# The order of VectorE's work in a Mamba-2 group loop, and the order of its ring of weight loads

## Chip, core and metric

The kernel runs on one core of one Trainium2 chip. The metric is the device time of one execution in microseconds (us). Before the change it is 2198.63 us, the median of three runs (2197.93 to 2201.19).

## The reference, cut to what matters

One layer over 256 latent tokens and 256 context tokens, width 2048, in float32: adaLN modulation and RMSNorm, a bidirectional Mamba-2 mixer (64 heads in 8 groups of 8, state 128), a gated residual, a second norm, and a two-level mixture of experts.

```python
mx = modulation(c, ada_w, ada_b)            # silu(c) @ w + b, cut in six
hx = modulate(rms_norm(x, g), mx[0], mx[1]) # and hc from ctx
z, xbc, dt = split(h @ w_in)                # per group of heads: z 512, x 512, B 128, C 128 columns
xbc = silu(centred_dwconv(xbc, conv_w, conv_b))   # three taps over time
# per direction: the context's final state, then the latents
w = (C B^T) * exp(cum_i - cum_j) * dt       # masked to the triangle
y = w @ x + (C * exp(cum)) @ state + D * x
y = rms_norm(y * silu(z), norm_g) @ w_out
x = x + mx[2] * y
x = x + mx[5] * hier_moe(modulate(rms_norm(x), mx[3], mx[4]))
```

`mx[2]` to `mx[5]` come from the last two thirds of `ada_w`; they are needed only after the mixer.

## The kernel before, in words

The stages, in order: a front (norms, the first third of `ada_w`, dt and the first projection), the group loop, the output projection, routing, and a loop over experts that streams their weights.

The group loop runs `steps(g, w, ssd)` on each engine, for g = 0 (only weights, `w`), 1 to 7 (weights of group g and the SSD work, `ssd`, of group s = g - 1) and 8 (SSD of group 7 beside the first output tiles). A group has ten weight chunks of 128 columns, `CHUNKS`: 0 is B, 1 is C, 2, 5, 8, 9 are x, and 3, 4, 6, 7 are z. B and x chunks are projected for 512 tokens, C and z for 256. Each chunk is 1 MB of `w_in`, loaded to one of the three slots of `raw`.

A float32 product is made of three passes in a rounded format: ScalarE copies the weights rounded (`conv_hi`, L706, tile `whi`), VectorE subtracts to get the residue (`conv_lo`, `lo`, L955, tile `wlo`), and TensorE (`project`, L1585 and L1586, then L1590) runs the high weights against both parts of the activations and then the low weights against the high part. `whi` and `wlo` have two slots each. ScalarE's first convolution tap (`conv_first`, L724) and VectorE's other two (L1098, L1101 in `drain`) leave PSUM; for z chunks `drain` is one multiplication (L1090). ScalarE takes a tanh, VectorE finishes the silu (`store`, L998).

Beside the chunks, in each group:
- The second and third part of the modulation: eight tiles "a" of `ada_w`, 1 MB each, in the same three slots. `ada_sum(g, j)` (L1226, L1229) multiplies a tile's four rows of columns into `arow` on VectorE; after four tiles TensorE's `ada_columns` (L1669) sums over the partitions, and VectorE's (L1235) adds the bias.
- The SSD work: `differences` (L1027, VectorE, 16 instructions), `decays` (L774 and L779, ScalarE's exponentials), `weights` (L1037 and L1041, VectorE), each in two halves; `scaled_x` (L1055 to L1058), `states` and `y_chunk` 0 to 3 on TensorE, `finish` (L1066 to L1072) on VectorE, and `y_stores` on GpSimd's queue.

Every engine's order within a step n is written out by hand. TensorE: chunk n, then `states` at step 2, `y_chunk` 0 and 1 at step 3, 2 and 3 at step 6. They wait for `weights` of the half (`s_wts`, `s_ce`). ScalarE: `conv_hi` of the next chunk first, then the decays at steps 0 and 4, then tanh and first tap. VectorE: `conv_lo` of the next chunk first, then the rest.

`LOADS` is the order in which SP issues the 18 loads of a group: ten "w" and eight "a". The one at position p takes slot p mod 3, and waits until the load three positions earlier is used up: a "w" by its `conv_lo` (`s_lo`), an "a" by its `ada_sum` (`s_aadd`). SP is in order, so a load also waits for those ahead of it. After the last group the same slots take tiles of `w_out`, and SP issues `y_load`, which brings back `yh` and `yl` (0.5 MB each per group), between them; the first output tile on TensorE (`out_tile`, L1688) waits for both parts of group 0. The second of them is issued when the last chunk of the loop is done.

Of the kernel before, what the change touches and what calls it, by code (L numbers as in the profile page):

```python
# [36 lines left out]
NCH = len(CHUNKS)  # L37
# [7 lines left out]
ADDS = [4 * j + 4 for j in range(NADA)]  # L45
NADD = ADDS[-1]

ADA_STEP = {0: 0, 1: 1, 2: 2, 3: 3, 5: 4, 6: 5, 7: 6, 8: 7}
LOADS = [("w", 0)] + [t for n in range(NCH - 1) for t in [("w", n + 1)] + ([("a", ADA_STEP[n])] if n in ADA_STEP else [])]
RAW = 3  # L50
SLOTS = 64

# [1 line left out]
def build(nc, t):  # L54
# [70 lines left out]
    with ExitStack() as ctx:  # L125
# [170 lines left out]
        s_prod = sem("s_prod")  # L296
# [364 lines left out]
        def _(act):  # L661
# [38 lines left out]
            def conv_hi(g, n):  # L700
                m = NCH * g + (n + 1)
                pos = POS[("w", n)]
                act.wait_ge(s_raw[raw_of(pos)], raw_count(group_raw(g), pos))
                if not (isinstance(g, int) and g == 0 and n == 0):
                    act.wait_ge(s_wh, m - 1)
                act.activation(whi[:, (n + 1) % 2, :], raw[:, raw_of(pos), :], ACT.Copy).then_inc(s_hi, 1)  # L706
# [74 lines left out]
            def steps(g, w, ssd):  # L781

                s = g - 1
                for n in range(NCH):
                    if w and n + 1 < NCH and not (isinstance(g, int) and g == 0 and n < 2):
                        conv_hi(g, n + 1)
                    if w and n + 1 == NCH:
                        if not (isinstance(g, int) and g == GROUPS - 1):
                            conv_hi(g + 1, 0)
                        else:  # L790
                            out_hi(0)
                    if not w and n == 0:
                        tanh_of(s, NCH - 1)
                        turn_store(s, 8)
                    if not w and n != 3:
                        out_hi(n + 1)
                    if not w and n == 2:
                        out_hi(4)
                    if ssd and n in (0, 4):
                        decays(s, n // 4)  # L800
                    if n > 0 and w:
                        tanh_of(g, n - 1)
                    if n == 0 and ssd and w:
                        tanh_of(s, NCH - 1)
                    if w and n in CONV_AT:
                        if not (isinstance(g, int) and g == 0 and n == 0):
                            conv_first(g, n)
                    if ssd and n == 0 and w:
                        turn_store(s, 8)
                    if ssd and n == 1:  # L810
                        turn_store(s, 9)
                    if ssd and n == 2:
                        act.wait_ge(s_st, s + 1)
                        act.activation(st[:, 0, :], STK[0][:, :], ACT.Copy)
                        act.activation(st[:, 1, :], STK[1][:, :], ACT.Copy).then_inc(s_stev, 1)
                    if w and n in (2, 4, 7):
                        turn_store(g, {2: 0, 4: 2, 7: 5}[n])
# [60 lines left out]
        def _(dve):  # L878
# [205 lines left out]
            def drain(g, n):  # L1084

                kind = CHUNKS[n][0]
                slot, bank = n % 2, banks[(n + 1) % 2]
                if kind == "z":
                    dve.wait_ge(s_win, NCH * g + (n + 2))
                    dve.tensor_scalar(cv[:, slot, 0:L], bank[:, 0:L], 0.5, None, ALU.mult).then_inc(s_drain, 1)  # L1090
                    return
                q = 2 if kind in "Bx" else 1
                o = cv[:, slot, 0:q * L].rearrange("p (q t) -> p q t", q=q)
                u = bank[:, 0:q * L].rearrange("p (q t) -> p q t", q=q)
                col = conv_col(g, n)
                i = NCONV * g + (CONV_AT[n] + 1)
                dve.wait_ge(s_cvA, i)
                dve.scalar_tensor_tensor(o[:, :, 1:L], u[:, :, 0:L - 1], tapc[:, 0, bass.ds(col, 1)], o[:, :, 1:L],  # L1098
                                         ALU.mult, ALU.add).then_inc(s_cvB, 1)
                dve.wait_ge(s_cvB, i)  # L1100
                dve.scalar_tensor_tensor(o[:, :, 0:L - 1], u[:, :, 1:L], tapc[:, 2, bass.ds(col, 1)], o[:, :, 0:L - 1],  # L1101
                                         ALU.mult, ALU.add).then_inc(s_drain, 1)
# [39 lines left out]
            def steps(g, w, ssd):  # L1142
                s = g - 1
                for n in range(NCH):
                    if ssd and w and n == 4:
                        finish(s, 0)
                        finish(s, 1)
                        differences(s, 1)
                    if w and n + 1 < NCH and not (isinstance(g, int) and g == 0 and n < 2):
                        conv_lo(g, n + 1)  # L1150
                    if w and n + 1 == NCH:
                        if not (isinstance(g, int) and g == GROUPS - 1):
                            conv_lo(g + 1, 0)
                        else:
                            out_lo(0)
                    if not w and n not in (0, 2, 3):
                        out_lo(n)
                    if not w and n == 1:
                        dve.wait_ge(s_ads, 2 * GROUPS)
                        dve.tensor_copy(a2c, adab[:, ADA1:ADA1 + ADA2]).then_inc(s_a2, 1)  # L1160
                        dve.wait_ge(s_a2, 1)
                        dve.scalar_tensor_tensor(a2c[:, 2 * KC:3 * KC], a2c[:, 2 * KC:3 * KC], 1.0, g1col, ALU.add, ALU.mult).then_inc(s_a2, 1)
                    if not w and n == 3:
                        dve.wait_ge(s_a2T, 1)
                        dve.tensor_copy(a2row, ADAK[0:ADA2, 0:P]).then_inc(s_a2r, 1)
                    if not w and n == 0:
                        store(s, NCH - 1)
                    if ssd and n == 0:
                        dve.tensor_copy(tokg[:, :, :, :], tokm[:, :, :, bass.ds(R * s, R)]).then_inc(s_tg, 1)
                        dve.wait_ge(s_prod, NCH * s + 2)  # L1170
                        dve.tensor_copy(cT2[:, :], cT[:, :]).then_inc(s_ct2, 1)
                        dve.wait_ge(s_tg, s + 1)
                        differences(s, 0)
                    if not w and n == 4:
                        finish(s, 0)
                        finish(s, 1)
                        differences(s, 1)
                    if w and n == 6:
                        ada_columns(g, 0)
                    if ssd and n == 7:  # L1180
                        finish(s, 2)
                        finish(s, 3)
                    if ssd and n == 0:
                        if w:
                            store(s, NCH - 1)
                        skip_term(s, 8)
                    if w and n > 0:
                        store(g, n - 1)
                    if ssd and n == 1:
                        skip_term(s, 9)  # L1190
                    if w and n == 4:
                        skip_term(g, 2)
                    if w and n == 7:
                        skip_term(g, 5)
                    if not w and n == 1:
                        out_lo(2)
                        scaled_x(s)
                        out_lo(3)
                    if ssd and w and n == 1:
                        scaled_x(s)  # L1200
                    if ssd and (n == 5 or (n == 1 and not w)):
                        weights(s, n // 5)
                    if w and n == 8:
                        masked(g)
                    if w and not (isinstance(g, int) and g == 0 and n == 0):
                        drain(g, n)
                    if isinstance(g, int) and g == 0 and n == 2:
                        dt_columns()
                    if w and n == 9:
                        ada_columns(g, 1)  # L1210
                    if ssd and w and n == 1:
                        weights(s, 0)
                    if w and n in ADA_STEP:
                        ada_sum(g, ADA_STEP[n])

            def ada_sum(g, j):
# [288 lines left out]
        def _(pe):  # L1505
# [187 lines left out]
            def steps(g, w, ssd):  # L1693
                s = g - 1
                for n in range(NCH):
# [25 lines left out]
                        y_chunk(s, 1 if n == 3 else 3)  # L1721
                    if w and n == 7:
                        c_times_b(g)
                    if w and n in (5, 9):
                        ada_columns(g, n // 9)

            steps(0, True, False)
            with pe.Fori(1, GROUPS - 1) as g:
# [164 lines left out]
```

## Time and profile before

| | us |
|---|---|
| median of 3 runs | 2198.63 (2197.93 to 2201.19) |
| profiled execution, span from first to last instruction | 2195.6 |
| TensorE busy | 1980.9 (90%) |
| VectorE busy | 1228.3 (56%) |
| ScalarE busy | 496.7 (23%) |
| GpSimd busy | 153.7 (7%) |
| mean rate of the DMA over the span | 304 GB/s |

The page gives no other time of the profiled execution than its span; the median of the runs lies 3.0 us above it, for what lies around the first and the last instruction. The group loop runs from about 133 to 997 us, the output projection to about 1205, the experts from about 1249 on. In the profile PE is TensorE's matmuls, DVE VectorE, ACT ScalarE, POOL GpSimd, SPq the queue from which SP issues loads. PEclk is the granted TensorE clock as a share of full speed. A number in brackets at the end of a timeline row is the idle time ahead of it, with what ended it.

### The profile page before, as it was taken

The page shows a single profiled execution, that of the slowest core. Times are in us where ns is not written, and L with a number is a line of the kernel's source. Part 1 is how long each engine was busy: PE and PEld are TensorE (multiplying, and loading weights), DVE is VectorE, ACT ScalarE, POOL GpSimd, SP SyncE. Part 2 cuts the span into 40 slices and gives each one's busy share as a digit, 9 for nine tenths or more (in the row PEclk, how much of TensorE's full clock was granted, in tenths as well). Part 3 has the DMA queues.
Part 4 walks back from the last instruction along what each step waited for, and adds up shares of the span by engine and source line. Part 5 has one row for each costly group of instructions (what it writes and reads, how often), then busy time and mean ns, then how long its engine had stood idle before and what let it go on. Part 6 is the DMA issues. An engine that isn't in the chain of part 4 may idle for free.

```text
span 2195.6 us, 27594 instructions
## 1 busy us (share of the span) xinstructions
PE 1980.9 (90%) x10090; PEld 1228.5 (56%) x10090; DVE 1228.3 (56%) x1999; ACT 496.7 (23%) x577; POOL 153.7 (7%) x214
## 2 busy tenths in 40 slices
PE   5768999999999999999998798999988889989888
PEld 2358788888787878787787533333333333333333
DVE  2367788888888888888784623333222233322234
ACT  3123333333333333335444300000000000000000
POOL 0000000000000000000691000000000000000000
PEclk9789999999999999999999899999999999999999
DMA  9958576767676767679672699999999999999997
GB/s 361 313 171 246 164 219 184 221 183 218 189 214 190 214 190 212 192 221 310 231 236 91 268 426 426 427 427 427 426 426 426 426 426 427 427 427 426 425 426 288
DMA packets 294718, 666.68 MB, mean 304 GB/s; under 512 B 13505, under 2 KB 188001, under 8 KB 261009
## 3 DMA queue, kind: packets, MB, share of 16 engines
q1 hardware_dynamic: 285728, 639.45, 78.1%
q0 software_dynamic: 7984, 26.40, 3.7%
q8 instruction: 28, 0.46, 0.1%
q10 hardware_dynamic: 960, 0.23, 0.1%
q14 instruction: 18, 0.14, 0.0%
HBM read 655.40 MB, written 10.65 MB: 303 GB/s over the span
## 4 chain that ended last, share of the span: by engine, by line
DMA 28%; PE 17%; POOL 4%; DVE 1%; issue 1%; SPq 1%; ACT 0%; DVEq 0%; POOLq 0%
DMA wt<-in_moe_w_up 28%; PE bank L1831 12%; PE bank L1688 2%; POOL ysq L638 1%; POOL ysq L645 1%; POOL ysq L643 1%; PE bank L1856 1%; SPq L529 1%; PE bank L1795 0%; PE bank L1796 0%; PE bank L1813 0%; PE bank L1747 0%; PE bank L1788 0%; PE bank L1740 0%; DVE x L1465 0%
## 5 line engine op out<-in xcount | busy, mean ns | idle before, releaser
L1831 PE MATMUL bank<-wt,xe 128*64 128x512 f32 x1984 | 468.0, 627 | 80.5 <-DMA wt<-in_moe_w_up 80.5
L1465 DVE TENSOR_TENSOR x<-x,bank 128x512 f32<-128x512 f32 x256 | 158.3, 680 | 536.0 <-PE bank L1813 536.0
L1585 PE MATMUL bank<-hTh,whi 128*128 128x256 f32 (+1 forms) x1264 | 408.0, 343 | 16.4 <-ACT whi L706 14.1
L1586 PE MATMUL bank<-hTl,whi 128*128 128x256 f32 (+1 forms) x1264 | 401.0, 337 | 0.0
L1831 PEld LDWEIGHTS bank<-wt,xe 128*64 128x64 f32 x1984 | 164.1, 144 | 381.0 <-issue 380.9
L1585 PEld LDWEIGHTS bank<-hTh,whi 128*128 128x128 f32 x1264 | 241.8, 191 | 47.6 <-ACT whi L706 15.9
L1590 PE MATMUL bank<-hTh,wlo 128*128 128x256 f32 (+1 forms) x1264 | 240.8, 346 | 18.3 <-DVE wlo L955 18.3
L1586 PEld LDWEIGHTS bank<-hTl,whi 128*128 128x128 f32 x1264 | 242.1, 192 | 23.6
L1590 PEld LDWEIGHTS bank<-hTh,wlo 128*128 128x128 f32 x1264 | 204.5, 199 | 44.5 <-DVE wlo L955 20.1
L1856 PE MATMUL bank<-wt,hdn 128*64 128x512 f32 x1024 | 226.8, 595 | 1.4 <-DVE hdn L1477 1.4
L706 ACT ACTIVATE whi<-raw 128x2048 fp32r<-128x2048 f32 x80 | 153.1, 1914 | 302.3 <-DMA raw<-in_ssm_w_in 285.0
L955 DVE TENSOR_TENSOR wlo<-raw,whi 128x2048 fp32r<-128x2048 f32 x80 | 183.0, 2288 | 60.4 <-ACT whi L706 60.1
L867 ACT ACTIVATE gsb<-bank 128x512 f32<-128x512 f32 x32 | 19.1, 597 | 835.9 <-PE bank L1831 835.9
L1229 DVE SCALAR_TENSOR_TENSOR arow<-raw,cvec,arow 128x512 f32<-128x512 f32 x240 | 180.0, 750 | 6.8
L1856 PEld LDWEIGHTS bank<-wt,hdn 128*64 128x64 f32 x1024 | 70.7, 137 | 153.0 <-issue 127.9
L1813 PE MATMUL bank<-osb,gTb 64*128 64x512 f32 x512 | 138.1, 622 | 1.7 <-DVE osb L1494 1.7
L965 DVE SCALAR_TENSOR_TENSOR wlo<-raw,packs,whi 128x512 fp32r<-128x512 f32 x128 | 113.5, 947 | 34.1 <-ACT whi L757 34.1
L1494 DVE TENSOR_TENSOR osb<-bank,gate_h 128x512 f32<-128x512 f32 x64 | 41.2, 685 | 109.3 <-PE bank L1856 109.3
L757 ACT ACTIVATE whi<-raw,packs 128x512 fp32r<-128x512 f32 x128 | 81.9, 712 | 81.8 <-issue 58.9
L1813 PEld LDWEIGHTS bank<-osb,gTb 64*128 64x128 f32 x512 | 53.5, 185 | 65.4 <-issue 48.2
L1688 PE MATMUL bank<-whi,yh 128*128 128x512 f32 x256 | 66.4, 402 | 4.4 <-issue 2.9
L774 ACT ACTIVATE wts<-wts 128x3072 f32<-128x3072 f32 x16 | 44.4, 2776 | 99.3 <-DVE wts L1027 99.3
(304 smaller groups left out, 1837.9 us busy)
## 6 DMA issues: line engine op xcount, KB each, us to landing
wt<-in_moe_w_gate SPq DMA_DIRECT2D x64, 2048.0 KB, 16.6
wt<-in_moe_w_up SPq DMA_DIRECT2D x64, 2048.0 KB, 21.1
wt<-in_moe_w_down SPq DMA_DIRECT2D x64, 2048.0 KB, 18.5
raw<-in_ssm_w_in SPq DMA_DIRECT2D x80, 1024.0 KB, 6.1
raw<-in_ada_w SPq DMA_DIRECT2D x70, 1024.0 KB, 6.2
raw<-in_ssm_w_out SPq DMA_DIRECT2D x32, 1024.0 KB, 5.1
fr<-in_ada_w SPq DMA_DIRECT2D x26, 1024.0 KB, 11.6
bc<-cum_d POOLq DMA_DIRECT2D x32, 512.0 KB, 4.9
```

The costliest lines, as they stand in the source:

```text
L706: act.activation(whi[:, (n + 1) % 2, :], raw[:, raw_of(pos), :], ACT.Copy).then_inc(s_hi, 1)
L955: dve.tensor_tensor(wlo[:, slot, :], raw_tile, whi[:, slot, :].bitcast(F32), ALU.subtract).then_inc(s_lo, 1)
L965: last = dve.scalar_tensor_tensor(wlo[:, m % 2, cols], raw[:, raw_of(OUT0 + i), cols], ngcol[:, 4 * q + j:4 * q + j + 1], whi[:, m % 2, co ...
L1229: dve.scalar_tensor_tensor(arow[:, :], tile[:, i, :], column, arow[:, :], ALU.mult, ALU.add).then_inc(s_aadd, 1)
L1465: dve.tensor_tensor(x1[:, tt, cols], x1[:, tt, cols], banks[(1, 3, 6, 7)[nb]][:, :], ALU.add).then_inc(s_acc2, 1)
L1585: pe.matmul(bank[:, 0:width], wh[:, k, :], hTh[:, k, 0:width], start=(k == 0), stop=False)
L1586: last = pe.matmul(bank[:, 0:width], wh[:, k, :], hTl[:, k, 0:width], start=False, stop=False)
L1590: last = pe.matmul(bank[:, 0:width], wl[:, k, :], hTh[:, k, 0:width], start=False, stop=(k == KC - 1))
L1688: last = pe.matmul(banks[2 * nb + tt][:, :], a[:, 4 * q + j, P * tt:P * tt + P], ring[:, m % 2, 512 * j:512 * j + 512], start=(q == 0 and ...
L1813: pe.matmul(banks[(1, 3, 6, 7)[nb]][:, :], gTb[rows, P * tt:P * tt + P], osb[rows, nb // 2, :], start=True, stop=True).then_inc(s_cm[nb % ...
L1831: last = pe.matmul(banks[0][SLOTS * h:SLOTS * h + SLOTS, :], rows[:, k, :], wt[2 * q + h][:, FF * i:FF * i + FF], start=(k == 0), stop=(k ...
L1856: last = pe.matmul(banks[4 + nb // 2][SLOTS * h:SLOTS * h + SLOTS, :], hdn[:, f, :], wt[2 * NQ + f // 2][:, D * (f % 2) + 512 * nb:D * (f ...
```

## The change

It touches the three orders and nothing that is computed. It adds one wait.

- `LOADS` is written out in another order: w0 w1 a0 w2 w3 a1 w4 a2 w5 w6 a3 w7 a4 w8 a5 w9 a6 a7, where it was w0 w1 a0 w2 a1 w3 a2 w4 a3 w5 w6 a4 w7 a5 w8 a6 w9 a7.
- ScalarE: `conv_hi` of chunk 6 moves from the start of step 5 to step 4, ahead of the second `decays`.
- VectorE: `ada_sum(0)` goes behind the first `differences` of step 0 (in group 0 it stays at the step's end). `conv_lo` of chunk 3 goes from the start of step 2 to the end of step 1, ahead of `ada_sum(1)`. In step 4, `drain` of chunk 4, `conv_lo` of chunk 6 and the second `weights` come right behind `conv_lo` of chunk 5 and ahead of the stores; `weights` were in step 5. `ada_sum` 3 to 7 move to steps 5, 6, 7, 8 and 9 (they were in 3, 5, 6, 7 and 8), those of steps 5 and 9 ahead of `drain`. The first `ada_columns` go to step 7 on VectorE and step 6, behind `y_chunk`, on TensorE.
- `drain` of a z chunk waits for the store two chunks back as well (`s_prod`).

```diff
-ADA_STEP = {0: 0, 1: 1, 2: 2, 3: 3, 5: 4, 6: 5, 7: 6, 8: 7}
-LOADS = [("w", 0)] + [t for n in range(NCH - 1) for t in [("w", n + 1)] + ([("a", ADA_STEP[n])] if n in ADA_STEP else [])]
+LOADS = [("w", 0), ("w", 1), ("a", 0), ("w", 2), ("w", 3), ("a", 1), ("w", 4), ("a", 2), ("w", 5),
+         ("w", 6), ("a", 3), ("w", 7), ("a", 4), ("w", 8), ("a", 5), ("w", 9), ("a", 6), ("a", 7)]
+ADA_STEP = {1: 1, 2: 2, 5: 3, 6: 4, 7: 5, 8: 6, 9: 7}
+COLS_AT = {6: 0, 9: 1}
...
 # ScalarE, steps
-                    if w and n + 1 < NCH and not (isinstance(g, int) and g == 0 and n < 2):
+                    if w and n + 1 < NCH and n != 5 and not (isinstance(g, int) and g == 0 and n < 2):
                         conv_hi(g, n + 1)
+                    if w and n == 4:
+                        conv_hi(g, 6)
...
 # VectorE, drain of a z chunk
                     dve.wait_ge(s_win, NCH * g + (n + 2))
+                    dve.wait_ge(s_prod, NCH * g + (n - 1))
...
 # VectorE, steps
-                    if w and n + 1 < NCH and not (isinstance(g, int) and g == 0 and n < 2):
+                    if w and n + 1 < NCH and n not in (2, 5) and not (isinstance(g, int) and g == 0 and n < 2):
                         conv_lo(g, n + 1)
+                    if w and n == 4:
+                        drain(g, 4)
+                        conv_lo(g, 6)
+                        if ssd:
+                            weights(s, 1)
...
                         differences(s, 0)
+                        if w:
+                            ada_sum(g, 0)
...
-                    if w and n == 6:
-                        ada_columns(g, 0)
                     if ssd and n == 7:
                         finish(s, 2)
                         finish(s, 3)
+                    if w and n == 7:
+                        ada_columns(g, 0)
...
-                    if ssd and (n == 5 or (n == 1 and not w)):
+                    if not w and n in (1, 5):
                         weights(s, n // 5)
...
+                    if w and n in (5, 9):
+                        ada_sum(g, ADA_STEP[n])
-                    if w and not (isinstance(g, int) and g == 0 and n == 0):
+                    if w and n != 4 and not (isinstance(g, int) and g == 0 and n == 0):
                         drain(g, n)
...
                     if ssd and w and n == 1:
                         weights(s, 0)
-                    if w and n in ADA_STEP:
+                    if w and n == 1:
+                        conv_lo(g, 3)
+                    if w and not ssd and n == 0:
+                        ada_sum(g, 0)
+                    if w and n in (1, 2, 6, 7, 8):
                         ada_sum(g, ADA_STEP[n])
...
 # TensorE, steps
-                    if w and n in (5, 9):
-                        ada_columns(g, n // 9)
+                    if w and n in COLS_AT:
+                        ada_columns(g, COLS_AT[n])
```

## Rows read from the trace of the kernel before

**Rows 1.** Busy time by stretch: window, length, engines busy, PEclk, DMA share, GB/s.

```profile
341.87:451.35 109.48, 104.20 (x625) 88.18 (x624) 91.56 (x141) 39.97 (x38) 6.54 (x12) 0.97 0.68 202
...
1250.00:2195.60 945.60, 856.64 (x3714) 306.83 (x3710) 280.77 (x498) 31.39 (x64) 0.00 (x0) 0.97 0.99 417
```

**Rows 2.** Waits in the loop, 232 to 997 us: total us, times, longest.

```profile
PE bank L1590 <- DVE wlo L955: 18.3, 7, 2.8
...
PE bank L1640 <- issue: 16.2, 7, 2.3
...
PE bank L1585 <- ACT whi L706: 2.0, 7, 0.6
```

**Rows 3.** TensorE's timeline, low part of chunks 3 and 4: start, us, what.

```profile
380.72 3.44 PE L1590 MATMUL bank<-hTh,wlo 128*128 128x256 f32 x16 [2.69 <-DVE wlo L955]
...
392.73 2.08 PE L1590 MATMUL bank<-hTh,wlo 128*128 128x256 f32 x16
```

**Rows 4.** Busy time by stretch, around four waits of TensorE (PE column first).

```profile
380.00:388.00 8.00, 7.28 (x56) 5.89 (x58) 6.60 (x9) 2.43 (x2) 0.00 (x0) 0.79 0.91 275
412.00:421.00 9.00, 6.67 (x55) 4.77 (x55) 8.74 (x9) 0.63 (x1) 0.00 (x0) 0.81 0.23 90
184.92:194.00 9.08, 9.08 (x40) 7.53 (x41) 5.83 (x6) 2.96 (x4) 0.00 (x0) 1.00 1.05 316
1150.00:1165.00 15.00, 8.72 (x32) 7.00 (x31) 5.90 (x10) 3.27 (x6) 9.27 (x12) 0.70 0.41 140
```

**Rows 5.** VectorE's timeline in that group.

```profile
355.61 0.69 DVE L998 SCALAR_TENSOR_TENSOR slx<-slx,cv 128x512 f32<-128x512 f32 x1 [5.15 <-ACT slx L745]
...
375.36 3.10 DVE L1229 SCALAR_TENSOR_TENSOR arow<-raw,cvec,arow 128x512 f32<-128x512 f32 x4
378.38 2.28 DVE L955 TENSOR_TENSOR wlo<-raw,whi 128x2048 fp32r<-128x2048 f32 x1
...
407.23 2.29 DVE L955 TENSOR_TENSOR wlo<-raw,whi 128x2048 fp32r<-128x2048 f32 x1 [1.26 <-ACT whi L706]
...
409.77 3.42 DVE L1037 TENSOR_TENSOR wts<-wts,cbm 128x1536 f32<-128x1536 f32 x2
```

**Rows 6.** ScalarE's timeline: second exponentials, and the copy for chunk 6.

```profile
400.03 2.78 ACT L774 ACTIVATE wts<-wts 128x3072 f32<-128x3072 f32 x1 [5.96 <-DVE wts L1027]
...
405.29 1.91 ACT L706 ACTIVATE whi<-raw 128x2048 fp32r<-128x2048 f32 x1
```

**Rows 7.** The group's loads (L481), issue to landing.

```profile
DMA to landing us min/median/max: 5.1/6.1/8.9
```

**Rows 8.** VectorE's timeline at the group's end: a tap of chunk 8, its store.

```profile
441.06 0.74 DVE L1098 SCALAR_TENSOR_TENSOR cv<-bank,tapc,cv 128x510 f32<-128x510 f32 x1
...
449.50 0.68 DVE L998 SCALAR_TENSOR_TENSOR slx<-slx,cv 128x512 f32<-128x512 f32 x1
```

**Rows 9.** Timeline of group 0: SP's loads, a copy on ScalarE, chunks 3 and 5.

```profile
133.77 0.37 SPq L481 DMA_DIRECT2D raw<-in_ada_w  x1
157.40 0.37 SPq L481 DMA_DIRECT2D raw<-in_ssm_w_in  x1
...
166.83 1.91 ACT L706 ACTIVATE whi<-raw 128x2048 fp32r<-128x2048 f32 x1 [11.70 <-DMA raw<-in_ssm_w_in]
...
168.80 0.58 PE L1585 MATMUL bank<-hTh,whi 128*128 128x256 f32 x1 [10.08 <-ACT whi L706]
...
184.92 0.50 PE L1585 MATMUL bank<-hTh,whi 128*128 128x512 f32 x1 [2.09 <-ACT whi L706]
```

**Rows 10.** After the loop: a `y_load`, two waits of TensorE, landings of `yl`.

```profile
996.70 0.37 SPq L492 DMA_DIRECT2D yl<-yl_d  x1
...
1000.82 2.07 PE L1688 MATMUL bank<-whi,yh 128*128 128x512 f32 x8 [2.86 <-issue]
...
1018.86 1.98 PE L1623 MATMUL bank<-xwf,btok 128*128 128x512 f32 x4 [0.86 <-DVE xtok L1058]
...
DMA to landing us min/median/max: 4.0/10.7/13.2
```

## The prediction

> **What bounds the kernel now.** I read the stages first [rows 1]. From 1250 us on, the expert loop keeps the DMA at 0.99 of its time and 417 GB/s. It starts when the stage before it ends and the change touches nothing in it, so what is won or lost earlier moves the end one for one. The group loop (eight groups; the last seven carry the SSD work of the group before them) costs 109.48 us a group: TensorE is busy 104.2 of them, VectorE 91.6, the DMA 0.68. TensorE bounds it, so only its waits can be won. The list of waits [rows 2] has three of TensorE in the loop, each seven times: for a low part `wlo` 18.3 us in all (2.6 each), ahead of `y_chunk` 16.2 (2.3), for a `whi` 2.0 (0.3). Together 5.2 us a group.
>
> The timeline shows a second price [rows 3]: the 16 low matmuls behind the first wait took 3.44 us, the same 16 of the next chunk 2.08. The granted clock was 0.79 over those 8 us and 0.81 around the `y_chunk` wait [rows 4], a piece at 1.2 in place of 2.4 GHz each time: 0.21 x 8 and 0.19 x 9, 1.7 us each. Over a whole group it is 0.97 [rows 1], 3.3 us. So the waits cost 5.2 + 3.3 = 8.5 us a group, and a group without them takes 101.0.
>
> The Trainium skill (TensorE: Matmul & The Clock Gate, HAM oscillation — how this bites in real kernels) says that a long enough operand wait drops the engine to half rate and that the loop pays the return each time; the trace agrees [rows 3, 4]. By waits alone seven groups would give 36 us; with the clock they give 60.
>
> Why the waits are there: VectorE, in order. In step 3 the residue of `z0` starts at 378.38, right behind an `ada_sum` that ran 375.36 to 378.46 [rows 5]; its copy `whi` was long done. TensorE waited for it. In step 5 the residue of chunk 6 waits 1.26 us for its `whi`, which ScalarE makes only after both exponentials [rows 6]; behind it stand the second `weights`, which free `y_chunk` 2 at 415.4.
>
> **The change, part by part.** I count from the start of a group's chunk 0 on TensorE (341.87 = 0). Without waits TensorE starts chunk 1 at 11.3, 2 at 17.5, `states` at 28.5, 3 at 32.1 (its low part at 36.0), y 0 and 1 at 38, chunk 4 at 42.5 (low 46.4), 5 at 48.8 (low 56.1), 6 at 60.6 (low 64.5), y 2 and 3 at 66.5, 7 at 71.0 (low 74.9), 8 at 78.0, 9 at 89.1, and ends it at 100.0. The times below add up start-to-start durations of the same group's timeline, a few of which stand in rows 5, 6 and 8.
>
> (a) `ada_sum(0)` moves in front of the store of the last chunk. VectorE idles 5.15 us there (at 355.61) [rows 5], so its 2.75 us are covered, if its tile has landed. The tile is now loaded after `ada_sum(7)` of the group before, issued about -0.8; with the median landing of 6.1 [rows 7] it is there at 5.3, `differences` end at 7.2. Cover holds.
>
> (b) `conv_lo(3)` goes ahead of `ada_sum(1)`, and `w3` is loaded right after `w2`. With (a), VectorE finishes the first `weights` at 29.6 instead of 33.5; the residue ends at 31.8, TensorE wants it at 36.0. The 2.6 us wait goes. Next behind: `ada_sum(1)` to 34.8, drain(2) to 36.7, then `ada_sum(2)`, whose tile follows `conv_lo(3)` in the ring: issued 32, landed 38.1. VectorE waits 1.4 us (new), ends at 41.1, and `conv_lo(4)` at 43.3 against 46.4.
>
> (c) Step 4: finish 0 and 1, second `differences` to 51.3, `conv_lo(5)` to 53.5 (wanted 56.1), drain(4), `conv_lo(6)` to 56, second `weights` (3.34 + 2.20) to 61.6; y 2 wants them at 66.5. ScalarE makes `whi` of chunk 6 before the exponentials: its load follows `conv_lo(4)`, 43.5 + 6.1 = 49.6, copy to 51.5, exponentials 51.5 to 56. The 2.3 us wait goes, and so does the 0.3 for a `whi` (ready at 51.5, wanted at 60.6). The smallest slack left is 2.6 us, at chunk 5.
>
> (d) The added wait of drain for `s_prod` names a store two chunks back, done more than 2 us before in every step walked here: nothing.
>
> (e) `ada_sum(7)` now ends in step 9 and TensorE's second `ada_columns` waits for it. TensorE leaves chunk 8 at 89.1; ScalarE's first tap 0.9, drain(8) 1.55, `ada_sum(6)` 3.0, residue of the next chunk 0 2.2, store 0.6, `ada_sum(7)` 3.0 [rows 5, 8]: 100.4, against 100.0. If `w0` lands later than the median (it shares the queue with `a7`), the residue starts later: 8.9 instead of 6.1 [rows 7] gives 2.5 us. Bounds 0.3 and 2.5; I take 0.8, near the median. Behind a wait of 2.09 us at 184.92 [rows 9] the granted clock was 1.00 [rows 4], so I add nothing for it. Each drain(9) and the next group's start then stand as before.
>
> (f) Group 0. TensorE waits 10.08 us for `whi` of chunk 3, because its load is issued only after `ada_sum(0)` (157.40) and lands at 166.7 beside two more [rows 9]. Now `w3` follows `conv_lo(1)` at 133.8, so chunk 3 starts behind drain(1) at 159.2. But the tiles `a1`, `a2`, `w4` come after `ada_sum(0)` as before, and `ada_sum(1)` and `ada_sum(2)` stand ahead of `conv_lo(4)`: 166.7 + 3.0 + 2.9 + 3.0 + 2.2 = 177.8, so chunk 4 waits about 4 us and ends at 179.7 to 180.7 (was 182.2). Chunk 5 then loses its 2.09 us wait. Gain 1.5 to 6, I take 3.
>
> (g) The end. The output phase's third weight tile takes the slot of `a7`, no longer of `w8`, and SP issues it before `y_load(0)`. Before, `y_load`'s second half went at 996.70, landed in 4.0 us, and TensorE started at 1000.82, 4.3 after its last chunk [rows 10]. Now `ada_sum(7)` of the last group also stands behind `out_lo(0)` (2.7 us, fed by a 2.5 us copy) and ends 2.5 us after the last chunk; then 1.05 MB of weights, 0.52 and 0.52 MB go out in a row. 2.1 MB at 417 GB/s [rows 1] is 5.0 us, some 5.6 with loads of two kinds mixed, plus the 2.6 that a 4.0 us landing leaves beside the 1.4 of its own 0.52 MB: TensorE starts 10.8 after its last chunk, 6.5 later; 0.86 of it is absorbed by the wait at 1018.86. Another idle stretch, 15 us of which TensorE worked 8.7, went with a granted clock of 0.70 [rows 4], so I add 1.5 to 3 for clock. Bounds: 0 (if `ada_sum(7)` were as early as `w8` before) and 10; I take 7.5.
>
> The DMA page of the Trainium skill (DMA: Bandwidth & Descriptors, Queues, rings and completion order) says that each DMA engine consumes a queue's descriptors in ring order, which speaks against this change: the small loads wait behind the megabyte. The `yl` rows agree, 4.0 us with nothing ahead and a median of 10.7 in the backlog. Were they independent, (g) would cost some 4 us in place of 7.5.
>
> **Sum.** Seven groups x -8.5 = -59.5; (e) in six, +4.8; (f) -3; (g) +7.5: -50.2 us. The profiled execution spans 2195.6, 3.0 under the median shown; the same difference goes on top: 2195.6 - 50.2 + 3.0 = 2148.4, 2148 us.
>
> **The rivals.**
> R1, the wait of (e) becomes a restart: `w0` lands late behind `a7` and the `bc` loads, TensorE waits 2.5 us and the clock falls (1.7), as at the two waits removed. 4.2 in place of 0.8, in six groups: +20, 2168. For: longest landing 8.9 in the group walked. Against: the median.
> R2, one of the two waits stays: slack 2.6 at chunk 5, 3.1 at chunk 4, both behind the ring's chain. One wait is 2.6 + 1.7: +30, 2178. For: (b) makes VectorE wait for `a2`. Against: 2 to 5 us of slack everywhere.
> R3, slower: the ring binds. `conv_lo(3)`, load `a2`, `ada_sum(2)`, `conv_lo(4)`, load `w6`, its copy, exponentials, `weights`, y 2 form one chain with two landings. It has 4.9 us to spare. If each landing took 13.2 as in the output phase's backlog [rows 10], it would end 14.2 late and TensorE would wait 9.3 in all, 4 at chunk 4 and 5.3 ahead of y 2, and lose 1.7 of clock twice: 12.7 against the 8.5 won, +4.2 in seven groups and +9.3 from (e) to (g): 2237. It decides from landings of some 11 us. Against: 8.9 at most here, and DMA at 0.68.
> R4, nothing moves: another wait of the same length appears, 2199. Nothing in the walk shows one.
>
> **Chances.** Forecast 0.75, R1 0.10, R2 0.08, R3 0.04, R4 0.03. Range 2135 (no cost in (g), 6 in (f)) to 2174 (R1, and half of R2). 0.2% is 4.4 us, about what this kernel's runs can tell from nothing: faster 0.93, same 0.03, slower 0.04.
>
> **What would show it.** Per group: 101 to 102 us; no TensorE wait for `wlo` and none ahead of `y_chunk`; a granted clock near 1.00 in the loop; a wait ahead of L1669's matmuls of 0.3 to 1 us, in the second `ada_columns` only; in group 0 chunk 3 at about 159 with a wait in chunk 4; an idle TensorE of 6 us or more ahead of the first output tile. The forecast is wrong if a group takes over 104 us, or if ScalarE's second exponentials start later than 52 after the group's start.

## The result, and the profile after

The changed kernel takes 2179.1 us (median of 4 runs, 2174.7 to 2182.6) against 2199.7 (four runs now, 2197.9 to 2201.2; the first three had 2198.6): a ratio of 0.9905, 95% interval 0.9893 to 0.9917. It is 20.6 us faster, where 50 were forecast, and outside the range given. The profiled execution spans 2173.2 us against 2195.6. It is the fastest of the four, 4.4 us below their median; the medians carry the result, the traces the account of it.

Both old waits of TensorE are gone: the list of its waits from 232 to 997 us (total us, times, longest) has one line of the loop, and it is a new one; the other is the first output tile.

```profile
PE bank L1687 <- DVE arow L1247: 22.9, 7, 3.5
PE bank L1706 <- issue: 6.5, 1, 6.5
```

L1687 is the second `ada_columns`, which waits for `ada_sum(7)`, 3.0 to 3.5 us in each of the last seven groups. The timeline of the end of one group (start, us, what; `...` stands for rows left out) shows how that wait comes about:

```profile
418.02 0.55 POOL L601 DMA_DIRECT2D bc<-cum_d  x1 [0.23 <-issue]
418.75 0.55 POOL L601 DMA_DIRECT2D bc<-cum_d  x1 [0.18 <-issue]
...
420.24 0.37 SPq L483 DMA_DIRECT2D raw<-in_ada_w  x1
...
422.47 9.74 SPq L483 DMA_DIRECT2D raw<-in_ssm_w_in  x2
...
428.57 3.11 DVE L1247 SCALAR_TENSOR_TENSOR arow<-raw,cvec,arow 128x512 f32<-128x512 f32 x4
...
432.24 1.92 ACT L708 ACTIVATE whi<-raw 128x2048 fp32r<-128x2048 f32 x1 [5.39 <-DMA raw<-in_ssm_w_in]
...
434.19 2.29 DVE L959 TENSOR_TENSOR wlo<-raw,whi 128x2048 fp32r<-128x2048 f32 x1 [2.52 <-ACT whi L708]
436.40 0.68 DVE L1002 SCALAR_TENSOR_TENSOR slx<-slx,cv 128x512 f32<-128x512 f32 x1
...
437.00 3.11 DVE L1247 SCALAR_TENSOR_TENSOR arow<-raw,cvec,arow 128x512 f32<-128x512 f32 x4
...
440.24 1.05 PE L1687 MATMUL bank<-ones,arow 128*128 128x1 f32 x8 [3.48 <-DVE arow L1247]
...
441.15 0.58 PE L1603 MATMUL bank<-hTh,whi 128*128 128x512 f32 x1
...
441.53 0.63 PE L1604 MATMUL bank<-hTl,whi 128*128 128x512 f32 x1
```

Read it from below. TensorE waits 3.48 us for the sum that VectorE began at 437.00. That sum stands behind a store and the residue at 434.19, and this residue idled 2.52 us for ScalarE's `whi`. ScalarE itself had waited for the load of `w0`, issued at 422.47: 9.8 us to the start of its copy. The same load took 7.7 before the change (issued 437.60, copy at 445.34). The load of `a7`, issued at 420.24, landed 8.4 us later, 8.3 ahead of its sum; VectorE can't reach that sum past the blocked residue.

What `w0` waited for stands in the DMA's view. A row of this weight chunk is 512 bytes long. From 422.5 to 426.5 no packet of that size moved (the packets below 2 KB are the 23 below 512 bytes):

```profile
DMA packets 489, 1.19 MB, mean 299 GB/s; under 512 B 23, under 2 KB 23, under 8 KB 489
...
q1 hardware_dynamic: 349, 0.71, 50.8%
q0 software_dynamic: 140, 0.48, 37.7%
```

SP's queue (q1) was moving `a7`, which `w0` stands behind, and GpSimd's (q0) took over a third of the engines' time beside it.

Behind the wait, TensorE runs slowly. Busy time by stretch (columns as in rows 1), the group and two starts of chunk 0:

```profile
335.12:441.15 106.03, 102.55 (x625) 87.10 (x624) 91.69 (x142) 40.13 (x37) 6.55 (x12) 0.98 0.70 208
...
441.15:444.55 3.40, 3.40 (x11) 2.62 (x11) 3.09 (x5) 0.00 (x0) 0.00 (x0) 0.53 0.92 296
```

A granted clock of 0.53 is the 1.2 GHz level, but for a remainder: matmuls of 0.63 us in place of 0.39. Chunk 0's high part takes 8.96 us instead of 7.36, so the wait costs 1.6 more. Without both the group would take 100.9, close to the 100.7 that e1 below measures.

**Where the 22.4 us of span come from**, taken between the second `ada_columns` of groups 0 and 7 (starts 231.44 and 996.51 before, 229.85 and 969.07 after): group 0 -1.6; seven groups 765.1 to 739.2, -25.9, or 109.3 to 105.6 each; from the last of them to the first output tile 4.3 to 8.1, +3.8; all that follows +1.2.

### The profile page after: what moved, and what is told of

Its sections match the earlier page's. It is cut to its first block, busy times and chain, and to the rows that moved or that the text cites. A ratio compares the mean times of both kernels' runs of the same rounds, so it can differ in the third digit from the quotient of the medians.

```text
span 2173.2 us, 27626 instructions
## 1 busy us (share of the span) xinstructions
PE 1974.7 (91%) x10090; PEld 1222.7 (56%) x10090; DVE 1229.5 (57%) x1999; ACT 498.0 (23%) x577; POOL 153.9 (7%) x214
## 4 chain that ended last, share of the span: by engine, by line
DMA 29%; PE 17%; POOL 4%; DVE 1%; issue 1%; SPq 1%; ACT 0%; DVEq 0%; POOLq 0%
DMA wt<-in_moe_w_up 29%; PE bank L1849 12%; PE bank L1706 2%; POOL ysq L640 1%; POOL ysq L647 1%; POOL ysq L645 1%; PE bank L1874 1%; SPq L531 1%; PE bank L1813 0%; PE bank L1814 0%; PE bank L1831 0%; PE bank L1765 0%; PE bank L1758 0%; PE bank L1806 0%; DVE x L1483 0%
## 5 line engine op out<-in xcount | busy, mean ns | idle before, releaser
L1603 PE MATMUL bank<-hTh,whi 128*128 128x256 f32 (+1 forms) x1264 | 413.7, 347 | 8.5 <-ACT whi L708 5.9
L1604 PE MATMUL bank<-hTl,whi 128*128 128x256 f32 (+1 forms) x1264 | 407.2, 342 | 0.0
L1608 PE MATMUL bank<-hTh,wlo 128*128 128x256 f32 (+1 forms) x1264 | 231.2, 335 | 0.2 <-DVE wlo L959 0.2
L1608 PEld LDWEIGHTS bank<-hTh,wlo 128*128 128x128 f32 x1264 | 196.8, 190 | 24.7 <-DVE wlo L959 0.4
L726 ACT ACTIVATE cv<-bank,tapc 128x512 f32<-128x512 f32 (+1 forms) x48 | 35.6, 742 | 169.7 <-PE bank L1608 134.3
```

What stands on the lines that cost most here:

```text
L1603: pe.matmul(bank[:, 0:width], wh[:, k, :], hTh[:, k, 0:width], start=(k == 0), stop=False)
L1604: last = pe.matmul(bank[:, 0:width], wh[:, k, :], hTl[:, k, 0:width], start=False, stop=False)
L1608: last = pe.matmul(bank[:, 0:width], wl[:, k, :], hTh[:, k, 0:width], start=False, stop=(k == KC - 1))
```

## The experiments

Every run was timed in three rounds beside the kernel before, whose medians were 2200.6 (first four) and 2198.7 (last four). "Period" is the mean over the seven groups of the profiled execution, between second `ada_columns`. After and e4 run the same code in the loop, so the 0.7 us between their periods is what two executions can differ by.

| kernel | median us | ratio, 95% interval | period us |
|---|---|---|---|
| before | 2199.7 | 1 | 109.30 |
| after | 2179.1 | 0.9905 (0.9893-0.9917) | 105.60 |
| last sum first (e1) | 2138.9 | 0.9721 (0.9704-0.9737) | 100.69 |
| `bc` loads later (e2) | 2162.4 | 0.9821 (0.9805-0.9837) | 103.79 |
| quarter of `a7` (e3) | 2129.9, not comparable | 0.9682 (0.9666-0.9699) | 102.87 |
| `y_load` first (e4) | 2174.5 | 0.9879 (0.9863-0.9896) | 106.31 |
| before + part (c) (p1) | 2175.1 | 0.9888 (0.9868-0.9908) | 105.24 |
| before + (b), old ring (p2) | 2216.9 | 1.0085 (1.0068-1.0101) | 111.36 |
| e1 without (a) (p3) | 2148.7 | 0.9773 (0.9756-0.9789) | 102.27 |
| e1 and e4 (e5) | 2136.8 | 0.9722 (0.9706-0.9738) | 100.69 |

### e1: `ada_sum(7)` ahead of the residue of the next group's chunk 0

```
                     if w and n + 1 == NCH:
+                        ada_sum(g, ADA_STEP[n])
                         if not (isinstance(g, int) and g == GROUPS - 1):
...
-                    if w and n in (5, 9):
+                    if w and n == 5:
                         ada_sum(g, ADA_STEP[n])
```

Expected: 

> Only VectorE's order in step 9 differs from the changed kernel: ada_sum(7) stands ahead of the residue of the next group's chunk 0 instead of behind it. Theory A (the new wait of 3.4 us ahead of the second ada_columns comes from the order: the sum is queued behind a residue that waits 2.5 us for its whi, whose load took 9.7 us): the sum ends about 2 us before TensorE's last chunk, the wait goes in all seven groups with the 1.6 us of clock behind it, a group takes 101 us, and the end's third weight tile comes earlier too: 2179 - 35 - 2 = about 2142. Theory B (the tile of the sum itself lands late, all loads at the group's end being slow): the wait stays at 1 us or more, 2165 or above.

Measured: 2138.9 us, 40 less than after, as theory A said. In the group's end of its trace both sums run back to back ahead of the residue:

```profile
418.23 8.71 SPq L483 DMA_DIRECT2D raw<-in_ssm_w_in  x2
...
423.30 6.26 DVE L1248 SCALAR_TENSOR_TENSOR arow<-raw,cvec,arow 128x512 f32<-128x512 f32 x8
427.49 1.92 ACT L708 ACTIVATE whi<-raw 128x2048 fp32r<-128x2048 f32 x1 [5.91 <-DMA raw<-in_ssm_w_in]
429.47 2.28 DVE L959 TENSOR_TENSOR wlo<-raw,whi 128x2048 fp32r<-128x2048 f32 x1
...
431.34 0.95 PE L1688 MATMUL bank<-ones,arow 128*128 128x1 f32 x8
```

`w0` is still late (9.3 us from issue to copy), and nobody waits for it: the residue ends at 431.75, and TensorE wants it at 439.51. 101 us around a group are filled without a gap at full clock:

```profile
330.00:431.00 101.00, 101.00 (x625) 86.31 (x624) 92.33 (x142) 40.02 (x37) 6.52 (x12) 1.00 0.74 219
```

So VectorE's order at the group's end is the cause of the missing gain: 4.9 us a group, 34 in the seven, and 2 more ahead of the first output tile. The profiled executions differ by 35.9 us, the medians by 40.2, since the one of after was 4.4 below its median.

### e2 and e3: why `w0` is late

e2 holds the `bc` loads of the next group back until ScalarE has made the copy fed by `w0`; e3 loads only a quarter of the tile of `ada_sum(7)`. e3 so computes another modulation, which sends tokens elsewhere: 1920 expert matmuls in place of 1984. Its total can't be compared; its groups can.

```
                 pool.wait_ge(s_ebc, 2 * s + 2)
+                pool.wait_ge(s_hi, NCH * s + (2 * NCH + 2))
                 load_bc(s + 1, 0)
```

```
+                    if kind == "a" and n == 7:
+                        sp.dma_start(a_view(raw_of(pos))[:, 0:1, :], src[:, 0:1, :]).then_inc(...)
+                        continue
```

Expected of e2: 

> The changed kernel, with GpSimd's queue issuing the two broadcast loads of bc for the next group (1 MB) only once ScalarE has copied the next group's chunk 0, so that they are not in flight beside the loads of a7 and w0. Theory C (these broadcasts make w0's landing 9.7 us instead of 6): it lands in 7 us or less, the wait ahead of the second ada_columns falls below 1 us, 2179 - 30 = about 2150. Theory D (it is a7 in the same ring, issued 2.3 us ahead): landing still about 9, 2175 to 2180. If both share it: about 8 us, wait 1 to 2, 2155 to 2170.

Expected of e3: 

> The changed kernel, with a7's load cut to one of its four rows of columns (three quarters of the tile are left out and the sum reads what the slot held; the last part of the modulation is wrong in the output). It is issued 2.3 us ahead of w0 in the same ring. Theory D: 0.79 MB less ahead of w0 is 2.4 us earlier, the wait falls to about 1 us and the clock's 1.6 come back, 2179 - 7 x 4 = about 2151. Theory C: w0 lands as late as before, 2175 to 2180.

Measured, the same load's issue and copy, and TensorE's wait, first e2:

```profile
424.27 9.73 SPq L483 DMA_DIRECT2D raw<-in_ssm_w_in  x2
...
430.90 1.92 ACT L709 ACTIVATE whi<-raw 128x2048 fp32r<-128x2048 f32 x1 [2.25 <-DMA raw<-in_ssm_w_in]
...
439.43 1.05 PE L1688 MATMUL bank<-ones,arow 128*128 128x1 f32 x8 [0.86 <-DVE arow L1248]
```

then e3:

```profile
420.78 9.73 SPq L486 DMA_DIRECT2D raw<-in_ssm_w_in  x2
...
428.79 1.92 ACT L711 ACTIVATE whi<-raw 128x2048 fp32r<-128x2048 f32 x1 [3.64 <-DMA raw<-in_ssm_w_in]
...
436.79 1.05 PE L1690 MATMUL bank<-ones,arow 128*128 128x1 f32 x8 [1.73 <-DVE arow L1250]
```

6.6 us in e2 and 8.0 in e3, against 9.8: in these groups the `bc` broadcasts account for 3.1 us and three quarters of `a7` for 1.8. So neither theory alone holds; 2162.4 lies in the range expected for a shared cause. No run takes both away. 9.8 less both is 4.9, near the 5.1 of the fastest load in rows 7, which leaves little for a third cause. The walk's 0.8 for step (e) was right for the landing it assumed: at 6.6 us the wait is 0.86. But other groups of e2 still wait up to 2.2, and it has a new wait, seen in its list of the loop's waits, because the held-back `bc` loads, issued at 433.53 and 434.26, now meet that of `w1` (433.63), which takes 9.2 us to land instead of 5.7, and VectorE's and ScalarE's work behind it comes late to the copy of chunk 2:

```profile
PE bank L1688 <- DVE arow L1248: 10.6, 8, 2.2
PE bank L1604 <- ACT whi L709: 3.5, 3, 1.2
```

Moving the loads gives back 1.8 us a group; moving one sum on VectorE gives 4.9.

### e4: `y_load(0)` ahead of the third output tile

```
+                if i == RAW - 1:
+                    sp.wait_ge(s_wh, M_OUT)
+                    y_load(0, 0)
+                    sp.wait_ge(s_win, M_OUT)
+                    y_load(0, 1)
                 if i < RAW:
...
                 sp.dma_start(a_view(raw_of(OUT0 + i)), w_out[...]).then_inc(...)
-                if i == RAW - 1:
...
```

Expected: 

> The changed kernel, with SP issuing both halves of the first y_load ahead of the third output weight tile. If the 7.2 us between the loop's last work on TensorE and the first output tile is the megabyte ahead in the ring, it falls back to about 3.5 to 4.5, and a piece at half clock goes: 3 to 6 us less, about 2175. If the wait has another cause (the stores of the rows themselves), it stays at 7 and the time at 2179.

Measured: 2174.5, 4.6 us less than after. After the loop SP of the changed kernel issued the megabyte first, and TensorE's first output tile waited (two views of after, SP's queue and TensorE):

```profile
969.04 0.37 SPq L507 DMA_DIRECT2D raw<-in_ssm_w_out  x1
969.52 0.44 SPq L494 DMA_DIRECT2D yh<-yh_d  x1
970.07 0.44 SPq L494 DMA_DIRECT2D yl<-yl_d  x1
...
977.20 3.32 PE L1706 MATMUL bank<-whi,yh 128*128 128x512 f32 x7 [6.54 <-issue]
```

In e4 both halves of `y_load(0)` go out at 967.97 and 971.60, before the weights at 974.30, and the tile starts right behind the loop:

```profile
974.33 1.05 PE L1687 MATMUL bank<-ones,arow 128*128 128x1 f32 x8 [2.76 <-DVE arow L1247]
975.24 0.63 PE L1631 MATMUL bank<-ident,slx 128*128 128x128 f32 x4
975.77 3.37 PE L1706 MATMUL bank<-whi,yh 128*128 128x512 f32 x8
```

So the wait was SP's order, as step (g) said: the first output tile starts 1.4 us behind the last `ada_columns` instead of 8.1. How much of these 6.7 us the kernel keeps isn't shown. What follows takes 1.2 longer, and the profiled spans are nearly equal, 2172.9 against 2173.2, since in e4's execution a group took 0.7 us more. The medians differ by 4.6, but the intervals of the two ratios overlap.

### p1: the kernel before with part (c) alone

ScalarE's copy of chunk 6, VectorE's drain, residue 6 and second `weights` move to step 4 as in the change; ring, residue 3 and sums stay.

Expected: 

> The kernel before with one part of the change alone, part (c): in each group the second set of decay weights is made behind the second exponentials, with ScalarE's copy of chunk 6's high weights and VectorE's residue of chunk 6 ahead of it; the old orders of the residues of chunks 3 and 4, of the sums of the modulation and of the weight ring stay. Theory (each of the two old waits of TensorE pays by itself): the second one goes, 2.33 us a group and 0.26 beside it, with the half-clock piece of 1.6 us behind it, 4.2 us a group, 7 groups: 2200.6 - 29 = 2171. Rival (the gain of this part is in the first wait's shadow, or the sum for chunk 7 becomes late also here): a gain of less than 10 us, 2190 or more.

Measured: 2175.1, no worse than the whole change. The loop's list has only the first old wait:

```profile
PE bank L1598 <- DVE wlo L957: 19.7, 9, 2.7
```

The period falls by 4.06 us, where waits and clock were priced at 4.2. 28.4 us in the groups; 1.6, 1.2 and 2.1 are given back in group 0, ahead of the first output tile and behind it.

### p2: part (b) with the old ring

```
-                    if w and n + 1 < NCH and not (isinstance(g, int) and g == 0 and n < 2):
+                    if w and n + 1 < NCH and n != 2 and not (isinstance(g, int) and g == 0 and n < 2):
                         conv_lo(g, n + 1)
...
+                    if w and n == 1 and not (isinstance(g, int) and g == 0):
+                        conv_lo(g, 3)
```

Expected: 

> The kernel before with VectorE's half of part (b) alone: the residue of chunk 3 goes ahead of the sum of the modulation for chunk 1, and the weight ring keeps its old order, in which the load of chunk 4's weights follows the release of that sum's buffer. Theory (order of the ring is needed for the order of VectorE): that load is issued 2.2 us later than before, its copy ends at about 388.8 us of the old profile where TensorE wants it at 384.3: TensorE waits some 4.5 us for the weights of chunk 4, instead of 2.7 for the residue: about 2210, no faster than before. Rival (VectorE's order alone does it): the wait and its clock go, 4.2 us a group: 2171.

Measured: 2216.9, slower than before. The residue runs earlier, but the sum of chunk 1, whose buffer chunk 4's weights take, now ends later (timeline, VectorE's residue and sum, SP, ScalarE, TensorE):

```profile
379.06 2.28 DVE L955 TENSOR_TENSOR wlo<-raw,whi 128x2048 fp32r<-128x2048 f32 x1
...
381.26 3.11 DVE L1233 SCALAR_TENSOR_TENSOR arow<-raw,cvec,arow 128x512 f32<-128x512 f32 x4
...
384.53 0.37 SPq L481 DMA_DIRECT2D raw<-in_ssm_w_in  x1
...
390.57 1.91 ACT L706 ACTIVATE whi<-raw 128x2048 fp32r<-128x2048 f32 x1 [12.22 <-DMA raw<-in_ssm_w_in]
...
392.53 0.58 PE L1589 MATMUL bank<-hTh,whi 128*128 128x256 f32 x1 [4.48 <-ACT whi L706]
```

4.48 us for `whi`, as worked out, in place of 2.6 for `wlo`. The total is 7 us above the 2210 expected: the seven groups lose 14.4 us, group 0 and what follows the loop another 4. VectorE's order and the ring's are one change: without its half in the ring the other half loses 2.1 us a group.

### p3: e1 without part (a)

```
                         differences(s, 0)
-                        if w:
-                            ada_sum(g, 0)
...
-                    if w and not ssd and n == 0:
+                    if w and n == 0:
                         ada_sum(g, 0)
```

Expected: 

> The version with the last sum of the modulation ahead of chunk 0's residue of the next group (2138.9 us), without part (a): the sum for chunk 0 goes back to the end of the step before, ahead of chunk 3's drain. Theory (VectorE's slack after part (b) is about as large as one sum, so part (a) is worth about 1.3 us a group): chunk 4 waits 0.8 us and chunk 5 1 to 2 us: about 2148. Rival (slack covers it): 2139, no change against that version.

Measured: 2148.7, 9.8 over e1, by a period 1.6 longer. No wait of over 0.4 us is left in its loop from 230 to 940 us, but 19 short ones, 5.1 us in all. In one group TensorE is idle 1.27 us, where e1's isn't idle at all:

```profile
330.50:433.50 103.00, 101.73 (x625) 86.07 (x623) 92.01 (x142) 39.95 (x38) 6.55 (x12) 1.00 0.72 214
```

That group takes 2.3 us longer than e1's; the part beyond the 1.27 isn't resolved by the profile, in which the ends of matmuls are modelled.

### e5: e1 and e4 together, the fastest version

Expected: 

> The version with the last sum of the modulation ahead of chunk 0's residue of the next group (2138.9 us), and with the load of the first y tile issued ahead of the third output tile after the loop, as in the run of that edit alone. Theory (the two are independent): the first output tile starts about 2 to 4 us sooner after the loop: 2135 to 2137. Rival (what is left of the wait after the loop is something else): 2139.

Measured: 2136.8 (2134.5 to 2139.4), beside e1's 2138.9 (2138.3 to 2139.7). The first output tile starts 4.2 us after the last `ada_columns` in place of 6.1, but the two sets of runs overlap. It beats after by 42 us and before by 62; nearly all of that is e1's.

## Why the prediction was wrong, step by step

**Right: what the two waits were worth.** With no wait left in the seven groups (e1) a group takes 100.69 us, 8.6 less than before; 8.5 was forecast, 5.2 of waits and 3.3 of clock. p1 shows the second wait by itself at 4.1.

**Right: (a), (b), (c), (d).** Neither old wait is left, and no other has come up between chunk 0 and chunk 9. In after, the residue of chunk 3 starts 31.3 us into the group (29.6 was said), the new wait of `ada_sum(2)` for its tile is 0.46 where 1.4 was said, and ScalarE's second exponentials start at 387.43, 52.3 into a group that begins at 335.12; 1.6 of that is the slow start of chunk 0. That passes the 52 which was to be the mark of a wrong forecast, and harmed nothing: the walk's slacks of 2 to 5 us held it. (a) is needed, as p3 shows (9.8 us), and so is the ring (p2).

**Wrong: (e), the second `ada_columns` waits for `ada_sum(7)`.** It was priced at 0.8 us a group, between bounds of 0.3 and 2.5, with nothing for the clock: +4.8 in six groups. It waited 3.0 to 3.5 us and cost 4.9 a group with the clock (after less e1), 34.4 in seven. The forecast had the last group's wait in (g); without its 3.5 the cost is 30.9 against 4.8, 26 of the 28 us by which the span missed. The mechanism was named, in the step and as R1 with 2.5 + 1.7 us; R1 got 0.10. Two choices failed. The landing of `w0` was taken at the median of the group's 18 loads, while this very load had taken 7.7 us, and the change itself puts `a7` ahead of it on the queue, beside the `bc` loads; it landed after 9.6, more than the 8.9 behind the upper bound. Step (g) reckoned with a queued megabyte after the loop; step (e) didn't a few lines earlier. Then the clock: it was left out because of the one wait of 2.09 us without a drop (rows 9), though waits of 2.3 and 2.7 us in the same trace had one (rows 4). So being 2.5 us wrong in the wait cost 4.1. Here a small error was not small.

The Trainium skill (DMA: Bandwidth & Descriptors, Queues, rings and completion order) says that each DMA engine switches in turn between the queue rows that hold work for it, a packet at a time; so a load on SP's queue gives up time to one from GpSimd though their queues differ. The trace agrees: in e2, with only the `bc` loads moved, `w0` needs 6.6 us instead of 9.8. Most of the difference passes through `a7`: `w0`'s first packet moves 4.1 us after its issue in after and 1.9 in e2.

**Half right: (f).** Group 0 gains 1.6 of the forecast 3: chunk 3 starts at 160.44 as said (about 159), but chunk 4 waits 5.89 where 4 was said.

**Right: (g).** The forecast counted from TensorE's last chunk, with the last wait for `ada_sum(7)` in it. That chunk ends at 965.60 in after, and the first output tile starts at 977.20: 11.6 us, where 10.8 was said, or 7.3 more than before. With the 1.2 behind it (g) costs 8.5 against 7.5, and e4 confirms the mechanism.

**The sum anew,** in the forecast's own terms: 7 x -8.6 = -60.3, (e) +30.9, (f) -1.6, (g) +8.5: -22.5, beside 22.4 measured in the span.

## What to carry to other kernels

On an in-order engine, don't queue work whose consumer is due now behind work that waits for a load and is due later: here one sum moved ahead of one residue is worth 36 us by the spans, 40 by the medians. When a walk gives a cost by a load's landing, take that load's own time and add what the change puts on the DMA ahead of it, not the median of all; and where the result is a wait of TensorE of 1 to 3 us, price it both with and without the clock. Two orders that share a ring of buffers (an engine's and the loads') must move together, or the buffer released later turns the gain into a loss.

## What the runs showed of the hardware

**A wait of TensorE can cost more than its length, and in these traces the length doesn't tell which one does.** The seven waits of 3.0 to 3.5 us in after were each followed by a piece at 1.2 GHz; five of 0.86 or 0.87 in e2 and e3 by none. Between them both happen. In e2 the same wait at the same place has two lengths in neighbouring groups. Behind 2.16 us the matmuls of the next chunk start at 0.63 us each, behind 0.86 at 0.39, and chunk 0's high part takes 10.2 us after the first, 2.8 more than after the second:

```profile
334.39 1.43 PE L1688 MATMUL bank<-ones,arow 128*128 128x1 f32 x8 [2.16 <-DVE arow L1248]
...
336.26 0.63 PE L1605 MATMUL bank<-hTl,whi 128*128 128x512 f32 x1
...
440.66 0.39 PE L1605 MATMUL bank<-hTl,whi 128*128 128x512 f32 x1
```

In e3 a wait of only 1.23 us came before such a piece, which cost 1.6 us; in p1 a wait of 2.68 us was followed by none, its 16 low matmuls taking 2.17 us where rows 3 has 3.44 behind 2.69. One row of each:

```profile
642.41 1.05 PE L1690 MATMUL bank<-ones,arow 128*128 128x1 f32 x8 [1.23 <-DVE arow L1250]
...
643.90 0.63 PE L1606 MATMUL bank<-hTh,whi 128*128 128x512 f32 x1
```

```profile
483.04 2.17 PE L1598 MATMUL bank<-hTh,wlo 128*128 128x256 f32 x16 [2.68 <-DVE wlo L957]
```

What else decides stays open.

**A load can stand still while the DMA as a whole is below its full rate.** In the 15 us around the late `w0` (418 to 433) the DMA moved 263 GB/s and was busy 0.84 of the time, against 416 and 0.99 in the expert loop, and a megabyte took 9.8 us in place of 5 to 6:

```profile
DMA packets 3240, 3.94 MB, mean 263 GB/s; under 512 B 144, under 2 KB 2219, under 8 KB 3240
...
q1 hardware_dynamic: 2760, 2.37, 50.4%
q0 software_dynamic: 480, 1.57, 33.2%
```

The software queue moved 1.57 MB in a third of the engines' time: 1.05 MB are the two `bc` broadcasts, 0.52 the four stores of `yh` and `yl` that GpSimd issued from 415.13 to 417.24. The last of these packets started at 425.2; `w0`'s first, behind `a7` in its own queue, at 426.6.
